# A fourth PSUM bank for the filler of a neighbourhood attention, and head sums that share the swapped tile's bank

## The reference

```
h    = rms_norm(x)
proj = h @ w_in            # q, k, v of 8 neighbourhood heads (64 wide each),
                           # q of 8 grouped heads, k and v of 2 shared heads
na   = softmax(q k^T / 8 + bias, masked) v               # the first attention
gq   = rope(rms_norm(q_grouped)); gk = rope(rms_norm(k_shared))
gqa  = softmax(gq gk^T / 8) v_shared                     # the second attention
x    = x + concat(na, gqa) @ w_out
```

## Time and profile before

| | us |
|---|---|
| median of 3 runs | 2090.17 (2087.02 to 2091.5) |
| the profiled execution | 2090.53 |
| its span | 2088.5 |
| TensorE busy (matmuls) | 1988.7 (95%) |
| VectorE busy | 1343.1 (64%) |
| ScalarE busy | 1087.9 (52%) |
| GpSimd busy | 157.6 (8%) |
| mean granted TensorE clock | 0.987 |

### The profile page before, as it was taken

One profiled execution on the slowest core, in us unless ns is written; L12 is line 12 of the kernel. 1 busy time (PEld: TensorE's weight loads), 2 busy tenths in 40 slices (PEclk: granted clock), 3 DMA queues, 4 the chain that ended last, 5 costly groups with the idle time before them and its releaser, 6 DMA issues.

```text
span 2088.5 us, 30500 instructions
## 1 busy us (share of the span) xinstructions
PE 1988.7 (95%) x12072; PEld 1737.5 (83%) x12072; DVE 1343.1 (64%) x2364; ACT 1087.9 (52%) x1854; POOL 157.6 (8%) x184
## 2 busy tenths in 40 slices
PE   7988899998989999999999999999999999999999
PEld 6867899887779987888997778888888998778887
DVE  5666687566658866555577786555555577686554
ACT  5555466455546654444555555445444555545443
POOL 1231000023200000000012200000000012300000
PEclk9999999999989999999999999999999999999999
DMA  6333366542324565556443235555555544225554
GB/s 254 121 112 121 103 198 226 185 146 92 131 91 162 184 199 180 184 181 191 149 162 123 85 121 184 188 179 178 195 184 183 167 157 138 85 92 186 188 181 131
DMA packets 90109, 329.91 MB, mean 158 GB/s; under 512 B 9968, under 2 KB 10352, under 8 KB 89584
## 3 DMA queue, kind: packets, MB, share of 16 engines
q1 hardware_dynamic: 89968, 327.97, 47.7%
HBM read 326.88 MB, written 1.05 MB: 157 GB/s over the span
## 4 chain that ended last, share of the span: by engine, by line
PE 77%; DVE 11%; ACT 7%; issue 2%; POOL 1%; DVEq 0%; ACTq 0%
PE PS L83 75%; DVE WL L98 3%; ACT WH L92 3%; PE PS L86 3%; DVE TMP L108 2%; ACT TMP L95 2%; DVE SM L114 1%; ACT TMP L94 1%; DVE TMP L98 1%; ACT TMP L92 1%; DVE GL L108 0%; DVE TMP L105 0%; DVE SM L108 0%; POOL SQ L111 0%; DVE X L98 0%
## 5 line engine op out<-in xcount | busy, mean ns | idle before, releaser
L98 DVE TENSOR_TENSOR WL<-RAW,WH 128x1024 fp32r<-128x1024 f32 x608 | 745.7, 1232 | 539.6 <-ACT WH L92 534.6
L92 ACT ACTIVATE WH<-RAW 128x1024 fp32r<-128x1024 f32 x608 | 641.3, 1057 | 547.5 <-PE PS L83 542.5
L83 PE MATMUL PS<-WH,GH 128*128 128x512 f32 (+1 forms) x912 | 360.1, 395 | 3.1 <-DVE WL L98 2.2
L83 PE MATMUL PS<-WH,GL 128*128 128x512 f32 (+1 forms) x912 | 353.1, 387 | 0.0
L83 PE MATMUL PS<-WL,GH 128*128 128x512 f32 (+1 forms) x912 | 352.5, 387 | 0.0
L83 PE MATMUL PS<-GH,WH 128*128 128x256 f32 x1104 | 320.6, 290 | 13.7 <-DVE WL L98 7.4
L83 PE MATMUL PS<-GL,WH 128*128 128x256 f32 x1104 | 315.3, 286 | 0.0
L83 PE MATMUL PS<-GH,WL 128*128 128x256 f32 x1104 | 315.1, 285 | 0.0
L83 PE MATMUL PS<-WH,HH 128*128 128x512 f32 (+1 forms) x736 | 278.9, 379 | 0.0
L83 PE MATMUL PS<-WH,HL 128*128 128x512 f32 (+1 forms) x736 | 276.4, 375 | 0.0
L83 PE MATMUL PS<-WL,HH 128*128 128x512 f32 (+1 forms) x736 | 276.3, 375 | 0.0
(11 more groups left out here) (140 smaller groups left out, 2371.2 us busy)
## 6 DMA issues: line engine op xcount, KB each, us to landing
RAW<-wts SPq DMA_DIRECT2D x608, 512.0 KB, 4.2
M<-bias SPq DMA_DIRECT2D x2, 2048.0 KB, 14.1
X<-x SPq DMA_DIRECT2D x2, 512.0 KB, 6.0
TMP<-mem SPq DMA_DIRECT2D x1, 1024.0 KB, 12.2
out<-X SPq DMA_DIRECT2D x4, 256.0 KB, 3.4
CST<-cst SPq DMA_DIRECT2D x1, 706.0 KB, 9.9
M<-gf SPq DMA_DIRECT2D x1, 512.0 KB, 6.7
PAR<-par SPq DMA_DIRECT2D x1, 368.0 KB, 7.5
```

What stands on the lines that cost most here:

```text
L83: return Issued(self.eng and self.eng.matmul(o, l, r, start=first, stop=last, skip_group_check=share))
L92: return Issued(self.eng.activation(o, i, f, scale=scale))
L98: return Issued(self.eng and self.eng.tensor_tensor(o, a, b, op))
```

## The change

Four things are changed, for both layers of the first block.

1. TensorE puts the head sums of a rope tile in columns 256 to 259 of the bank that its swapped tile then fills from column 0. The bank is now taken, and waited for, ahead of the sums. Bank 7 is not taken for sums.
2. All of the filler's tiles may now use banks 0 to 2 and bank 7 (`WT + STB`).
3. VectorE reads the head sums in its `rope(m)`, two instructions of 2 columns a tile ahead of the sine product, in place of two instructions of 10 columns in `rope_scales`, which now begins with Newton's first instruction.
4. ScalarE has rates of its own, `NA_PARTS`, and five more steps. Square and copy of a tile are split from the memory products that follow them. Rope tile 0 is squared and copied at the end of round 1 rather than after the exponentials of round 2, tile 2 at the end of round 2 rather than after the exponentials of round 3, and tile 4 at the end of round 3 rather than in round 4. In each case ScalarE does it ahead of that round's `high`.

```
+        NA_PARTS = [3, 3, 3] + [1, 1, 1] + [1, 2, 1] * 2 + [1, 1, 1]
...
                 def rope(m):
                     e.wait_ge(squared, ("rope", L, m))
-                    if m == 0:
-                        take(("rs", L), STB)
+                    ps = take(("sw", L, m), WT + STB)
                     for t in range(2):
-                        o = t * 10 + 2 * m
-                        i = e.mm(PS[7][:, o:o + 2], SQ[:, m % 3, t * 128:t * 128 + 128], cc(C_BL, 2), True, True)
+                        o = S + 2 * t
+                        i = e.mm(ps[:, o:o + 2], SQ[:, m % 3, t * 128:t * 128 + 128], cc(C_BL, 2), True, True)
                     i.then_inc(summed, ("rope", L, m))
-                    ps = take(("sw", L, m), WT)
...
-                        fm_tile(("rope", L, m), mix, WT)
+                        fm_tile(("rope", L, m), mix, WT + STB)
...
                         rope(m)
+                        if m % 2 == 0:
+                            yield
                         if m < 4:
                             memory(2 * m)
                             memory(2 * m + 1)
+                        if m % 2 == 1:
+                            yield
...
-                run(attention(("na", L), na_heads(L), [256, 256], fill, NA_RATES))
+                run(attention(("na", L), na_heads(L), [256, 256], fill, NA_PARTS))
...
                     e.wait_ge(spread, key)
+                    if m == 0:
+                        e.wait_ge(small)
+                    for t in range(2):
+                        o = 10 * t + 2 * m
+                        e.ts(smc(o, 2), bank(key)[:, S + 2 * t:S + 2 * t + 2], RX2[:, t:t + 1], EPS, ALU.mult,
+                             ALU.add).then_inc(small)
                     e.tt(tb[:, 256:512], bank(key)[:, 0:S], cc(C_SIN, S), ALU.mult).then_inc(dout, key)
...
                 def rope_scales():
-                    e.wait_ge(summed, ("rope", L, 4))
-                    e.wait_ge(small)
-                    v3 = smc(0, 20).rearrange("p (t n) -> p t n", t=2)
-                    for t in range(2):
-                        m = e.ts(v3[:, t, :], PS[7][:, t * 10:t * 10 + 10], RX2[:, t:t + 1], EPS, ALU.mult, ALU.add)
-                    m.then_inc(dout, ("rs", L))
-                    e.wait_ge(dout)
                     y3 = newton(20).rearrange("p (t n) -> p t n", t=2)
```

More of the change, by code:

```diff
@@ L634, in others @@
                 def others():
-                    yield from tm_wide(("v", L), mix, 512, WT)
+                    yield from tm_wide(("v", L), mix, 512, WT + STB)
                     for m in range(2, 4):
-                        fm_tile(("nk", L, m), mix, WT)
+                        fm_tile(("nk", L, m), mix, WT + STB)
                         yield
                     for m in range(5):
-                        fm_tile(("rope", L, m), mix, WT)
+                        fm_tile(("rope", L, m), mix, WT + STB)
                         if m >= 1:
@@ L643, in others @@
                         yield
-                    fm_tile(("gv", L), mix, WT)
+                    fm_tile(("gv", L), mix, WT + STB)
                     rope(4)
                     yield
-                    fm_tile(("mk", L, 0), mkv, WT)
-                    ps = take(("gvt", L), WT)
+                    fm_tile(("mk", L, 0), mkv, WT + STB)
+                    ps = take(("gvt", L), WT + STB)
                     e.wait_ge(ready, ("gv", L))
@@ L653, in others @@
                     yield
-                    fm_tile(("mk", L, 1), mkv, WT)
+                    fm_tile(("mk", L, 1), mkv, WT + STB)
                     yield
```

## The result

| | before | changed |
|---|---|---|
| median, us | 2088.86 (4 runs, 2087.02 to 2091.5) | 2076.64 (4 runs, 2075.27 to 2077.39) |
| profiled execution | 2090.53 | 2075.27 |
| its span | 2088.5 | 2073.2 |
| mean granted clock | 0.987 | 0.992 |

The ratio is 0.9940, with a 95% interval of 0.9923 to 0.9957: the change makes the kernel faster by 12.2 us between the medians, and by 9 to 16 us by the interval. Timed again beside the later experiments, it gave 2078.35 against 2090.71, ratio 0.9943 (0.9931 to 0.9955). I had forecast 2080.0, that is 10.1 us of gain.

What follows compares the result with a forecast made beforehand. TensorE bounds the kernel, busy 1988.7 of 2088.5 us. Layer gains of 5.2 and 6.2 make 11.4; with 2.4 for the clock in place of 3.75, 10.1; 2090.17 less 10.1 is 2080.0, range 2076.5 to 2085.7.

Steps and rivals of the forecast that it cites:

- The two waits for squares: TensorE's waits of 1.12 and 1.11 us at the sums behind rope tiles 1 and 3 go, worth 1.40 each.
- The price of the small reads: VectorE's two new reads of head sums per tile: taken as 0.30 us, bounds 0.26 and 0.84.
- The case of dear reads: Rival in VectorE's rope: two reads cost 0.84 us, making the new wait long, up to 2085.7; chance 0.15.
- Tile 4 gets a free bank: With four banks rope tile 4 takes tile 2's bank and starts at 81.26 instead of 86.42 us.
- the bank would not relieve it: Rival at tile 4: its new bank is not free either, start no earlier than 85.55, 2088.4 us; chance 0.07.
- The new wait: TensorE waits 1.3 us for VectorE's product of swapped tile 1, ahead of the sums behind tile 4; no clock fall.
- the long wait: Rival ahead of the sums behind tile 4: wait of 2.4 us and the clock falls, 2085.7 us; chance 0.15.
- none: Rival ahead of the sums behind tile 4: no new wait, 1.4 us more gain a layer, 2077.2; chance 0.07.
- The key scale's wait: TensorE's wait of 1.98 us for GpSimd at the spreading of the key's scale stays at about 1.9.
- The clock in the sum: Lower clock behind tile 4's old wait: 3.75 us in the profiled execution, counted as 2.4 by seven elevenths.
- The rule of the Trainium skill: Clock falls only behind longer idle times, so tile 4's slowness isn't the wait's: gain 7.65, 2082.5 us; rival's chance 0.07.
- the case of falls in more places: Rival for the whole kernel: shifted work makes the clock fall behind eight more waits, 15.2 us lost, 2095; chance 0.04.

Runs made afterwards that it cites:

- three added executions: The unchanged kernel before, profiled three more times to see how often the clock falls at tile 4; single executions 2091.84, 2091.94 and 2090.76 us.
- the order alone: Only ScalarE's new order put into the kernel before, with head sums in bank 7 and three filler banks as before; 2085.62 us, ratio 0.9977.
- three banks: The full change, but the filler has only banks 0 to 2 and bank 7 lies idle; 2085.17 us, ratio 0.9974 to the kernel before.

## Where the prediction was right, and which terms were mis-sized

- **The two waits for squares**: right. Each was worth 1.40 up to the next place where TensorE is held for another reason (a lock, from here on); the sums behind tile 1 and tile 3 came where the schedule had them.
- **The price of the small reads**: 0.26 a pair, taken as 0.30. The case of dear reads fell. The prediction counts six other reads off the chain; by its own schedule four are left, since those of tile 0 and tile 1 are in it. No number hangs on that.
- **Tile 4 gets a free bank**: right, without a wait in both layers. That the bank would not relieve it fell.
- **The new wait**: right in place, 1.12 instead of 1.3 us, and the clock did not fall behind it. Both ends, the long wait and none, fell.
- **The key scale's wait**: 1.77 instead of 1.9.
- **The attention as a whole**: predicted 5.2 and 6.2 shorter; the profiles show 5.4 (65.64 to 60.25, the second profile of the changed kernel) and 6.4 (66.71 to 60.29). Together 11.8 against my 11.4.
- **The clock in the sum**: the term that was mis-sized. The step read: "Seven elevenths of the mean of 1.9, twice, is 2.4 in place of 3.75." I had pooled all waits of about 2 us in the kernel. This is the step that failed. The three added executions show that behind this one the fall is regular, eight of eight, and costs 2 x 2.02 = 4.0: the sum had it 1.6 us too small. With it the sum is 11.4 - 3.75 + 4.0 = 11.7, against measured 12.2 and 12.4, and the forecast would have been 2078.5.
- **The clock behind the key scale's wait**: a term that the sum put at nothing. The wait stays, but the fall behind it came in 8 of 8 cases at 1.96 to 1.98 us and in 3 of 4 at 1.77 or 1.78, at 1.5 us each. On average that is 0.75 us of gain for the kernel, from four cases only.
- **The base**: not a mechanism. I subtracted from 2090.17; the kernel before had 2088.86 once a fourth run was in, and 2090.3 and 2090.7 on the later occasions. 1.3 of the 3.4 us are this. With both this and the clock term as measured the forecast would have been 2077.2.
- **The rule of the Trainium skill** (page "TensorE: Matmul & The Clock Gate", section "Why this matters for your kernels"): by it no fall was to be expected behind such waits, and a gain of 7.65. Eight falls of eight behind a wait of 2.12 us speak against it, as does the gain; the measurement decides.
- **What is left**: some 0.5 us. The falls behind the key's scale are of that size; "elsewhere" moves by more by itself, so this is argued and not shown. The profiled pair differs by 15.3 us: 10.7 in the attentions, 1.3 ahead of the first score matmul, and 3.3 elsewhere, of which 1.5 is the fall behind the key's scale that did not come in layer 0. Whether the rest is the change's is not shown.
- **The clock elsewhere**: the case of falls in more places did not come. Behind waits of 1.5 us or more the clock fell 12 to 14 times in the four profiles before, 8 and 11 times in the two of the changed kernel. Why it falls where it does stays open.

## What to carry to other kernels

A wait that is removed moves the work up to the next lock, not to the end: here two waits a layer of 1.40 each were worth 1.46 us together ahead of a late bank, 1.4 us behind the new ring, and 2.2 with the lock gone. A longer ring of buffers only buys time for a late consumer; look first at why it is late. VectorE had an idle stretch (1.58 us) in front of the conversion in the step of tile 1, and putting each product one filler step earlier made the fourth bank needless and took out two more waits: 2070.7 against 2076.6 to 2078.4. And when a stall is priced with the clock that falls behind it, take several executions of that same stall, not other stalls of the same length, and look behind the stalls that stay, too.

## What the runs showed of the hardware

- A pair of VectorE instructions of 128x2 with a PSUM source takes 0.26 us to the next instruction, and is busy 0.34; two of 128x10 were busy 0.36. The number of columns hardly counts at this size.
- Waits of about the same length differ in what the clock does behind them. Behind the wait of 2.12 us at tile 4, which has one of 1.11 some 3.7 us before it (82.72 and 86.42), it fell in eight of eight; behind the longer waits there with the order alone and with three banks (3.39 to 3.89), which have no other shortly before, in four of four; behind that of 2.16 at 818.40 it did not the earlier trace rows, in none of four executions; behind the new one of 1.12 it did not, in both profiles and both layers. Whether the earlier wait has a part in it is not shown.
- Behind the wait of 1.77 or 1.78 for GpSimd it differed from case to case. Windows of the changed kernel's first profile, layer 0 and then layer 1 (the eighth column is the clock):

```profile
101.10:104.50 3.40, 3.33 (x28) 3.33 (x28) 2.19 (x4) 0.00 (x0) 0.01 (x1) 1.00 0.49 164
...
486.30:489.00 2.70, 2.70 (x14) 2.70 (x14) 1.04 (x2) 0.00 (x0) 0.00 (x0) 0.50 0.53 185
```
